# In-projection groups in seven products from ready weight parts, in a two-layer hybrid trunk in float32

## What is computed

```python
for l in range(DEPTH):                       # DEPTH = 2
    h = _rmsnorm(x, norm_gain[l])
    proj = jnp.einsum('bsd,de->bse', h, w_in[l])           # 2048 -> 4352
    q, k, v, g_attn, x_rnn, g_rnn = jnp.split(proj, splits, axis=-1)
    attn = _swa_sink_attention(q, k, v, sinks[l], cos, sin)
    xc = _causal_conv(x_rnn, conv_w[l], conv_b[l])
    rnn = _rg_lru(xc, w_rgate[l], b_rgate[l], w_igate[l], b_igate[l], lru_param[l])
    mixed = jnp.concatenate([attn * jax.nn.silu(g_attn), rnn * jax.nn.silu(g_rnn)], axis=-1)
    x = x + jnp.einsum('bse,ed->bsd', mixed, w_out[l])     # 2048 -> 2048
return _rmsnorm(x, final_gain)
```

## Time and profile before

| | |
|---|---|
| median of three runs | 2304.1 us |
| the profiled execution | 2304.23 us, of which span 2301.7 us |
| granted TensorE clock | 1.0 throughout |
| TensorE, VectorE, ScalarE, GpSimd busy | 2292.8, 1565.0, 1339.1, 32.3 us |
| DMA traffic | 287.48 MB, mean 125 GB/s |

### The profile page before, as it was taken

The page is one execution under the profiler, slowest core; times in us unless marked ns, Lnnn a source line. Parts: engine busy times, 40 slices in busy tenths (PEclk is TensorE's granted clock), DMA queues, the critical chain, the costliest instruction groups (busy, mean ns, idle before and its releaser), DMA issues.

```text
span 2301.7 us, 36298 instructions
## 1 busy us (share of the span) xinstructions
PE 2292.8 (100%) x13798; PEld 1919.3 (83%) x13798; DVE 1565.0 (68%) x2546; ACT 1339.1 (58%) x2564; POOL 32.3 (1%) x58
## 2 busy tenths in 40 slices
PE   9999999999999999999999999999999999999999
PEld 8877888899888888889888888888988888888898
DVE  7658868656646877856675786885565478778555
ACT  7557666445546857645564676763455557666444
POOL 1110000000000000000000000000000000000000
PEclk9999999999999999999999999999999999999999
DMA  8886334545333233344534333344543333333444
GB/s 259 237 243 174 88 92 120 152 138 139 96 93 98 86 89 92 96 145 139 163 110 152 111 95 89 96 139 138 142 131 96 97 91 86 93 92 96 117 136 152
DMA packets 141389, 287.48 MB, mean 125 GB/s; under 512 B 16416, under 2 KB 20768, under 8 KB 138784
## 3 DMA queue, kind: packets, MB, share of 16 engines
q1 hardware_dynamic: 138096, 259.91, 38.1%
q0 software_dynamic: 2688, 25.17, 4.5%
q10 hardware_dynamic: 432, 0.10, 0.0%
HBM read 276.73 MB, written 33.55 MB: 135 GB/s over the span
## 4 chain that ended last, share of the span: by engine, by line
PE 96%; DVE 2%; DMA 1%; ACT 1%; issue 0%; DVEq 0%; POOL 0%; ACTq 0%; POOLq 0%
PE proj L682 80%; PE proj L703 10%; PE ps_at L811 2%; DMA wall<-in_w 1%; PE ps_at L786 1%; PE ps_at L830 1%; PE proj L722 1%; ACT wcut L905 0%; DVE wcut L1307 0%; PE proj L749 0%; PE ps_at L640 0%; DVE mixed L1791 0%; DVE acc L1402 0%; ACT operand L942 0%; PE ps_at L764 0%
## 5 line engine op out<-in xcount | busy, mean ns | idle before, releaser
L682 PE MATMUL proj<-operand,wcut 128*128 128x512 f32 x8376 | 1944.0, 391 | 1.3 <-DVE xr L1558 1.3
L682 PEld LDWEIGHTS proj<-operand,wcut 128*128 128x128 f32 x8376 | 1563.7, 188 | 337.9 <-issue 10.3
L1307 DVE TENSOR_TENSOR wcut<-wall,wcut 128x512 fp32r<-128x512 f32 x871 | 600.1, 689 | 582.0 <-ACT wcut L905 575.1
L905 ACT ACTIVATE wcut<-wall 128x512 fp32r<-128x512 f32 x870 | 548.3, 630 | 547.2 <-DMA wall<-in_w 381.0
L703 PE MATMUL proj<-xsum_out,wcut 128*128 128x256 f32 x1104 | 136.8, 283 | 0.0
L703 PEld LDWEIGHTS proj<-xsum_out,wcut 128*128 128x128 f32 x1104 | 134.9, 192 | 0.6
L703 PEld LDWEIGHTS proj<-operand,wcut 128*128 128x128 f32 x828 | 105.3, 191 | 3.9 <-DVE proj L1371 0.3
L703 PE MATMUL proj<-operand,wcut 128*128 128x256 f32 x828 | 106.6, 283 | 0.0
L1011 ACT ACTIVATE gy<-proj 32x512 f32<-32x512 f32 x144 | 85.1, 591 | 26.6 <-PE proj L682 22.1
L1102 ACT ACTIVATE sqr<-ps_at,pars 64x512 f32<-64x512 f32 x64 | 43.9, 685 | 91.8 <-PE ps_at L830 91.4
L1063 ACT ACTIVATE prob<-ps_at,stat 128x128 f32<-128x128 f32 x256 | 90.1, 363 | 0.8
(11 more groups left out here) (173 smaller groups left out, 1520.6 us busy)
## 6 DMA issues: line engine op xcount, KB each, us to landing
wall<-in_w SPq DMA_DIRECT2D x710, 256.0 KB, 2.6
wall<-weight_sums SPq DMA_DIRECT2D x92, 256.0 KB, 2.7
weight_sums<-in_blocks POOLq DMA_DIRECT2D x36, 512.0 KB, 6.5
wall<-in_blocks SPq DMA_DIRECT2D x69, 256.0 KB, 2.6
x<-in_xt SPq DMA_DIRECT2D x16, 512.0 KB, 3.8
mixed<-in_xt SPq DMA_DIRECT2D x14, 512.0 KB, 6.7
weight_sums<-weight_sums POOLq DMA_DIRECT2D x12, 512.0 KB, 5.2
gw<-in_gates SPq DMA_DIRECT2D x32, 128.0 KB, 2.6
```

The source lines that it names most:

```text
L682: last = pe.matmul(bank_of(l, 2 * g + m)[:, :], wcut[:, n % RING, a, c:c + P], operand[:, k, b, :], start=(i == 0 and k == 0), stop=(k == ...
L905: act.activation(wcut[:, u % RING, 0, :], wall[:, u % RING, 1, :], ACT.Copy).then_inc(w_hi, 1)
L1307: dve.tensor_tensor(wcut[:, u % RING, 1, :], wall[:, u % RING, 1, :], wcut[:, u % RING, 0, :].bitcast(F32), ALU.subtract).then_inc(w_lo, 1)
```

## The change

The in-projection's groups 7 to 15 are done in seven products in three stages: 7 to 15 in both layers of the second half, and 12 to 15 in layer 2 of the first half (22 groups). Four things come with it.

- **Ready parts.** While the first half does these groups, the split parts (high and low, 512 KB a unit) are stored to DRAM in `weight_cuts`, 142 units. In the second half a unit with ready parts is loaded whole (512 KB instead of 256 KB), and is neither cut by ScalarE nor by VectorE; TensorE waits for the load itself. Groups 7 to 15 of layer 1 and 7 to 11 of layer 2 have 7 ready units of 11 (the four built from sums are still split on the chip), groups 12 to 15 of layer 2 all 11. So that the parts match, the first half multiplies groups that are not in seven products in "block" units: the same 12 matmuls of 128x512, with weights taken by blocks.
- **SyncE.** Storing unit u+2 is issued after the load of unit u+6; before that load SyncE waits until the store of unit u has landed.
- **Sums.** GpSimd builds 10 more batches: layer 2's during the start of layer 2 of the first half, after the last out-projection batch, layer 1's from the start of the second half (`OPENS`).
- **x.** In the three stages the operands' sums lie over the residual `x`; at the start of layer 2 it is stored to `x_kept` (four stores of 1 MB) and read back from slot 127 on. Two odd recurrence tiles of the first half are read from their banks four slots earlier (`XR_EV`).

```diff
-IN_SEVEN = {(0, 0): (), (0, 1): (), (1, 0): (), (1, 1): ()}
+IN_SEVEN = {(0, 0): (), (0, 1): range(12, IN_LAST + 1), (1, 0): range(7, IN_LAST + 1), (1, 1): range(7, IN_LAST + 1)}
...
-BATCH.sort(key=lambda batch: batch[1] < PG)
-CUT_AT, READY, STORED = {}, set(), []
-SPLIT_NO = {n: n + 1 for n in range(TOTAL + UPG - RING)}
+BATCH.sort(key=lambda batch: (batch[1] < PG, batch[1] < PG and -batch[0]))
+KEYS = []
+CUT_AT = {}
+for n, (h, l, kind, g, j) in enumerate(UNIT):
+    if h == 0 and zone_of(g) == "in" and g in BUILT[l] and (kind, j) != ("block", WHOLE[A21]):
+        CUT_AT[key_of(l, kind, g, j)] = n
+        KEYS.append(key_of(l, kind, g, j))
+READY = {n for n, (h, l, *unit) in enumerate(UNIT) if h > 0 and key_of(l, *unit) in CUT_AT}
+STORED = sorted(CUT_AT.values())
+SPLIT = [n for n in range(TOTAL + UPG - RING) if n not in READY]
+SPLIT_NO = {n: i + 1 for i, n in enumerate(SPLIT)}
...
-XR_EV = [[slot_of("xr", j) + (6, 2)[h] * (j % 2) for j in range(RT)] for h in range(HALVES)]
+XR_EV = [[slot_of("xr", j) + (2 if h or j > RT - 4 else 6) * (j % 2) for j in range(RT)] for h in range(HALVES)]
...
+T_AT[0, 1, "in"] = (6, 7, 9, 11)
...
+OPENS = {5: (0, 1, 1), 11: (1, 0, 4)}
...
+        cuts = nc.dram_tensor("weight_cuts", (len(KEYS), P, 2 * KU * GW), F32).ap()
...
+                if n in READY:
+                    from_n = CUT_AT[key_of(l, kind, g, j)]
+                    sp_.wait_ge(cut_out[from_n % RING], 16 * stores_through(from_n))
+                    sp_.dma_start(wcut[:, n % RING, :, :].rearrange("p a c -> p (a c)").bitcast(F32),
+                                  cuts[KEYS.index(key_of(l, kind, g, j))]).then_inc(w_in[n % RING], 16)
+                    return
                 sp_.dma_start(wall[:, n % RING, 1, :], source(at)).then_inc(w_in[n % RING], 16)
...
                                 sp_.wait_ge(unit_done, u + 1)
+                                if u in STORED:
+                                    sp_.wait_ge(cut_out[u % RING], 16 * stores_through(u))
                                 w_load(u + RING)
+                            if u + 2 in STORED:
+
+                                sp_.wait_ge(w_lo, SPLIT_NO[u + 2])
+                                sp_.dma_start(cuts[KEYS.index(key_of(l, *UNIT[u + 2][2:]))],
+                                              wcut[:, (u + 2) % RING, :, :].rearrange("p a c -> p (a c)").bitcast(F32)
+                                              ).then_inc(cut_out[(u + 2) % RING], 16)
...
+                if n in OPENS:
+                    pool.wait_ge(built[S4], 32 * n - 16)
+                    add(S4, n - 1, A12)
+                    pool.wait_ge(unit_done, at_unit(*OPENS[n]))
...
-                pe.wait_ge(w_lo, SPLIT_NO[n])
+                if n in READY:
+                    pe.wait_ge(w_in[n % RING], 16 * (n // RING + 1))
+                else:
+                    pe.wait_ge(w_lo, SPLIT_NO[n])
```

More of the change, by code:

```diff
@@ L167, with stores_through @@
          if (g - max([0] + [n + 1 for n in range(g) if n not in BUILT[l]])) % 2 == 0]
-BATCH.sort(key=lambda batch: batch[1] < PG)
-CUT_AT, READY, STORED = {}, set(), []
-SPLIT_NO = {n: n + 1 for n in range(TOTAL + UPG - RING)}
+BATCH.sort(key=lambda batch: (batch[1] < PG, batch[1] < PG and -batch[0]))
[9 more added lines that the diff above has]
+SPLIT_NO = {n: i + 1 for i, n in enumerate(SPLIT)}
 X_BACK = [(h, l) for h in range(HALVES) for l in range(DEPTH) if l == 0 or (h, l, "in") in ZONES]
+def stores_through(n):
+    return sum(m % RING == n % RING for m in STORED if m <= n)
 def tile_of(what, t):
@@ L320, in build @@
         built = {n: sem(f"built{n}") for n in SUMS}
+        cut_out = [sem(f"cut_out{i}") for i in range(RING)]
         kept = [sem(f"kept{i}") for i in range(4)]
@@ L622, in _ @@
                     add(S3, n, A21)
-                if before:
+                if before and n not in OPENS:
                     pool.wait_ge(built[S4], 32 * n - 16)
```

## The result

The changed kernel takes 2317.45 us (median of 6 runs, 2311.21 to 2322.76) against 2304.23 us before: 1.0057 of it, 95% interval 1.0043 to 1.0071. It is slower by 13 us, where 2295 was forecast. The profiled execution is the longest of the six, 2322.76 us with a span of 2320.9 us, so lengths read from its trace add up to more than the difference of the medians.

What follows compares the result with a forecast made beforehand. TensorE's own time was taken to set the end: 2304.2 - 16.1 (seven products) + 5.0 (tight place) + 1.4 (ScalarE's order) + 0.5 (batches beside stores) = 2295.0 us. The range was 2287.5 to 2309 us.

Steps and rivals of the forecast that it cites:

- 0.73 was forecast from the out-projection: TensorE, each of 22 in-projection groups: 21.00 us in seven products against 21.73 plain, 16.1 us removed in all.
- The operand sums: VectorE, three more stages: 13.5 us of sums and cuts each, covered by the run-ahead; cost nothing.
- the stores beside plain groups: First half: a 512 KB store lands in 3.8 us, under the 5.4 us of two plain units; no cost.
- the tight place: Groups 12 to 15 of layer 2, first half: bandwidth, SyncE and VectorE meet; 5 us lost, bounds 0 and 12.
- chain of SyncE: Groups 12 to 15, first half: one store landing per two units, 3.8 to 4.4 us, giving 1.9 to 2.2 us a unit.
- wrong in kind: Failure sign: groups 7 to 15 of the second half not shorter, or the first half losing more than 12 us.
- 358 GB/s as a core's limit against HBM: Groups 12 to 15, first half: if the limit held for long stores, the time would be 2298; chance 1 in 20.
- stores move at the rate of the batches: Rival, groups 12 to 15, first half: loads and stores together reach only 270 GB/s; 2315 to 2325 us, chance 0.13.
- They hold up nobody: More batches of weight sums in layers 2 and 1: sums are ready, or nearly, when needed; no delay.
- ScalarE's order: Other 18 groups: the lead copy back ends slot 6's work, slack 1.5 us or more; 1.4 us lost, bounds 0 and 9.
- The 0.5 us of the first stage: First half near 160 to 178 us: batches overlap stores of parts; 0.5 us lost, bounds 0 and 2.
- isn't the trouble: VectorE in the second half: busy 168.89 of 221 us, and the change takes 1.0 us a group off it.

Runs made afterwards that it cites:

- e5: Changed kernel with layer 2's batches of weight sums opened 13 slots later, after the four stores of x: 2324.64 us.
- e1: Changed kernel without seven products in layer 2 of the first half, nor that stage's store of x and operand sums: 2290.22 us.
- e3: Changed kernel with each store of parts issued one unit earlier (unit u+3 after unit u, not u+2), same traffic: 2304.56 us.
- e2: Changed kernel storing no parts in groups 12 to 15 of layer 2, first half; seven products kept, second half splits these on the chip: 2301.27 us.
- e4: Changed kernel with layer 1's batches of weight sums opened at the out-projection of layer 2, first half, not at the second half's start: 2334.08 us.
- e6: Changed kernel without first-half seven products, batches moved: layer 1's to layer 2 of the first half, layer 2's to slot 14 of the last stage: 2288.40 us.
- e7: As e6, but no part stored and none loaded ready; the second half's groups 7 to 15 are split on the chip: 2306.01 us.
- e9: As e6, but two of layer 2's five batches open at slot 128 of the second half's first stage, three at slot 14 of its last: 2287.91 us.

## Why the prediction was wrong

**What was right.** TensorE sets the end, and the second half's groups got shorter: 8.4 us for nine groups, 0.93 each, where 0.73 was forecast from the out-projection. I haven't found why a group saves 0.2 us more here. The operand sums cost nothing (e5), nor did the stores beside plain groups (e1), and the tight place was named, with its chain of SyncE. The prediction also said what would make it wrong in kind, a loss of more than 12 us in the first half, and that came.

**The tight place, the term mis-sized.** It was set at 5 us with an upper end of 12. It cost 16.0 us by the groups' lengths and the 3.7 us that they should have saved: about 20. The failed step is the price of a link in SyncE's chain, above all the landing time. I took a 1 MB store's 5.1 us, one alone in its neighbourhood, took off the transfer of half of it and got 3.8 us, 4.4 at most. Beside plain groups that was right enough, as the issues of the changed kernel between 180 and 340 us show; in the tight place (888 to 948 us, second row), with other stores and loads under way, it was 4.7 us at the median:

```profile
weight_cuts<-wcut SPq DMA_DIRECT2D x46, 512.0 KB, 4.0
```

```profile
weight_cuts<-wcut SPq DMA_DIRECT2D x23, 512.0 KB, 4.7
```

From link to link it is 5.18 us, since SyncE's own 0.43 us between landing and next store counts too, and the prediction had put it at nothing. The chain allows exactly two units for it. One more unit took 7.9 us off these groups (e3). The second slip is in the same place: 411 GB/s over 3 us and 387 of loads alone were taken as the rate for 90 us of loads and stores. With the longer chain e3 moved 334 over 90 us there:

```profile
872.00:962.00 90.00, 81.37 (x598) 71.22 (x597) 70.74 (x117) 65.65 (x120) 0.00 (x0) 0.98 0.94 334
```

The Trainium skill, DMA: Bandwidth & Descriptors, Specifications, gives some 358 GB/s as a core's limit against HBM, to which the prediction gave 1 in 20. The 334 lie below it, but no run shows a limit there: e2 moved 376 GB/s over the 20 us from 587 on (loads, stores of `x` and copies within DRAM):

```profile
587.00:607.00 20.00, 19.41 (x84) 15.43 (x83) 11.88 (x16) 5.40 (x7) 2.13 (x3) 1.00 1.04 376
```

**A rival with the right number.** The prediction's "stores move at the rate of the batches" had 2315 to 2325 us at 0.13, and 2317 was measured, with 305 GB/s over the tight place. That is luck, as its cause isn't the runs': the engines could do more than its 270 GB/s (326 in e3's window), the four groups lost about 20 us where it had 33, and the rest of the loss came from waits that have nothing to do with the stored parts.

**The batches, the step that failed.** "They hold up nobody" asked only whether the sums would be ready. It left out what the batches do to others: with them the DMA engines are at 0.88 before anything is added. Beside them a 1 MB store lands in 8.5 to 16.1 us instead of 5.1. I applied this to 18 us in the first stage and not to the two places where new or needed stores meet the batches: the stores of `x` (5.2 us, cost at nothing) and the stores of the output (11.6 us in the profiled execution, not considered, since they were no part of the change). e4 and e5 show both from the other side: without batches beside them these losses are gone, at the output's stores in e6, e7 and e9 too.

**ScalarE's order and the first stage.** 1.4 us was taken for the copies back; in the last stage there is no such loss, groups 7 to 9 take 24.49 us each. The 0.5 us of the first stage is below what this stage varies by.

**The ready parts** I called worth nothing in themselves, and left VectorE in the second half at "isn't the trouble". With ready parts that is so; e7 shows that it holds only because of them.

**The clock.** TensorE's granted clock was 1.0 before, as long as it had matmuls. Here it falls for a time, after stalls, to 1.2 GHz, the lower of its two levels (1.2 and 2.4 GHz), for which the prediction had no price. A piece of the chain at the second place, and the window over it:

```profile
1301.63 8.53 PE proj L720 x24
```

```profile
1297.00:1311.00 14.00, 9.86 (x49) 7.73 (x42) 13.58 (x23) 7.72 (x12) 3.90 (x6) 0.76 0.67 170
```

After 4.1 us of idle time 24 matmuls take 8.53 us, 355 ns each on average instead of 226. That is 3.1 us more, on the chain, and a part of this place's 11.6. The mean clock of the whole execution is 0.996, which is 9 us of 2321 at worst, a part of it in the stalls themselves. In the tight place the chain is of stores, so the 0.97 there counts for little.

In sum, the spans differ by 19.2 us. By stages: the first is 2.4 us shorter, within what it varies by; the second 24.2 longer (16.0 in the tight place, 5.2 beside the stores of `x`, the rest in single groups); the third 5.1 longer (11.6 beside the stores of the output and 1.0 in group 2, less what groups 7 to 15 save); the last 8.4 shorter; and 0.7 at the end.

## What to carry to other kernels

Price a wait for a landing by the landing time under the load that the change itself makes, not by the median of a quiet kernel, and add the queue's own time between two links. One unit more in the chain took 7.9 us off the tight place. A background transfer that nobody waits for can still be the cause: check each of its stretches against every transfer that somebody does wait for, the old ones too. And put bulk work beside stretches whose loads have the most time to land (plain groups) and that have no other large transfer, not simply where the mean DMA share is low.

## What the hardware showed that I had not expected

- A 1 MB store that lands in 5.1 us landed in 8.5 to 16.1 beside accumulating DRAM copies, at a DMA share of 0.92 and 260 GB/s. A 256 KB load took 6.5 to 11.0 at the median of such places instead of 2.6, and single ones 12 to 17.
- Loads and stores of parts together moved 305 GB/s over 109 us when held back by their chain; with one more unit in it 326, and 355 in 20 us of that.
- After a stall of 4.1 us the same matmuls ran at 355 ns instead of 226 on average for 8.5 us, with a mean granted clock of 0.76 over the 14 us around it.
- Execution times spread more: 11.6 us for the changed kernel over six runs, 2.3 us for the kernel before beside it, 5.9 over 21 runs later. Full DMA engines alone don't explain it, since e7, which stores nothing, spreads by 9.3 us over 11.
